# Token order of the activations, dropped meta columns, and the x rows at the start, in a one-layer hybrid mLSTM/HGRN2/RWKV-7 step

## The chip, the cores and the metric

The kernel runs on one core of one Trainium2 chip. The metric is the device time of one execution in microseconds (us). Engines are named as in the profile: PE is TensorE's matmuls, PEld its weight loads, DVE is VectorE, ACT ScalarE, POOL GpSimd, SP the queue from which all DMAs are issued.

## The reference

A layer is run over three streams of tokens: 64 sample tokens, 16 learned meta tokens that stand ahead of the prompt, and 512 prompt tokens. The width is 2048. Cut to what matters here:

```python
h = rmsnorm(x, p['norm_pre'])
proj = h @ p['w_in']                    # branches A (mLSTM), B (HGRN2), C (RWKV-7), and merge gates
ya, state = mlstm_branch(pa, ...)       # h * sigmoid(og) * silu(z), 8 heads
yb, state = hgrn_branch(pb, ...)        # 4 heads
yc, shift, state = rwkv_branch(pc, ...) # token shift, 8 heads of 64
ga, gb, gc = split_cols(jax.nn.sigmoid(f32(pg)), G_SIZES)
merged = ga * (ya @ w_proj_a) + gb * (yb @ w_proj_b) + gc * (yc @ w_proj_c)
y = merged @ p['w_out']
return x + rmsnorm(y, p['norm_post']), states
...
y_prompt = x_p[:, N_META:]              # the rows of the meta tokens are dropped
```

The meta tokens act on the recurrent states and on the shifted row of branch C. Their own gates, projections and output rows are computed by the reference and then dropped.

## The kernel before

The 592 tokens stand in the order sample (64), meta (16), prompt (512). **Activations** are kept transposed, `xh` and `xl`: 16 slices of 128 features by 592 tokens, split into a high part of type float32r and the rest. Each **tile** of weights is 128 output columns: `w_raw` (2 buffers) is loaded by SP, ACT makes `whi` (`split_hi`, L1130), DVE `wlo` (`split_lo`, L1445). `product(n)` (L641 to L658) multiplies a tile: for each of 16 slices k, three combinations (`whi`,`xh`), (`whi`,`xl`), (`wlo`,`xh`), and each in two halves of 296 tokens, which is 96 matmuls of 296 columns. The result lies in one of two accumulators of two banks (`acc`), columns 0 to 295 and 512 to 807; an ACT operation over both halves (`plain`, L1138) takes it out.

There are 154 tiles: 1 for the mLSTM gates, 1 for the RWKV ranks, then 8 for each of 8 mLSTM heads (key, value, query, output gate, z, three merge gate tiles), 8 for each of 4 pairs of RWKV heads (k, r, v, z, four gate tiles), 6 for each of 4 HGRN heads (forget, query, value, z, two gate tiles), 16 of the projections (L1093, three banks) and 16 of the output. Which small matmuls of the recurrences stand between or inside the products of a tile is written out by hand (`stages`, a plan of block numbers for RWKV and HGRN). Gate logits and branch rows are stored to DRAM and read again in the projection stage.

**Start.** SP issues the loads of 5 blocks of x rows, then two weight tiles. ACT squares and sums each block as it comes (L1149), then takes Ln (L1151) and Exp (L1153) for all five reciprocal roots; DVE makes five diagonal matrices of them (L1461, `unit`), and PE turns the rows by a float32 matmul with such a matrix (L679, 5 for each of 16 slices, in a ring of 4 PSUM buffers). ACT and DVE make `xh` (L1158) and `xl` (L1466) of each. ACT and DVE split weight tiles 0 and 1 ahead of that. The product of tile 0 starts when slice 12 of `xl` is there, and after all turning.

The names of the banks in the rows: `acc` are the accumulators, `branch` the two other PSUM tensors, `act_hi`/`act_lo` are `xh`/`xl`, `w_hi`/`w_lo` the split weights, `scratch` is everything carved out of one large tensor (the x rows and the recurrences' buffers).

## Time and profile before

| | |
|---|---|
| median of 3 runs (lowest, highest) | 2520.03 us (2518.99, 2521.3) |
| the profiled execution, its own time | 2519.03 us |
| its span | 2517.1 us |
| PE busy | 2417.9 us, 96% |
| PEld, DVE, ACT, POOL busy | 93%, 43%, 29%, 4% |
| DMA moved | 221 MB, 88 GB/s in the mean |

The page lists for each group of instructions the line, the engine, the operation, the tiles it writes and reads, the shapes, the count, and the busy time with the mean of one; the idle time behind it is what the engine waited just before. Spans of matmuls overlap, as they are pipelined, so the pace of a stream of matmuls is read from the starts in the timeline or from the chain, not from the length of one.

### The profile page before, as it was taken

Reading aid. Unit: us, or ns where it says so; the run is one execution under the profiler, and the core shown is the slowest. Engines: PE = TensorE matmul, PEld = TensorE weight load, DVE = VectorE, ACT = ScalarE, POOL = GpSimd, SP = SyncE. Lnnn points to the kernel's source line nnn. Section 1 sums busy time; section 2 is a strip of 40 time slices with the busy share of each in tenths; the row PEclk is TensorE's granted clock in tenths of the full one; section 3 lists DMA queues with packets and bytes.
Section 4 is the critical chain, followed back from the end, with each engine's and each line's share of the span. In section 5 each row is a group of like instructions: output and inputs, shape, how many; then the busy total and the mean of one; then the engine's idle time right before and its main releaser. Section 6 shows DMA issues by size and latency. Waiting matters only on the chain.

```text
span 2517.1 us, 46160 instructions
## 1 busy us (share of the span) xinstructions
PE 2417.9 (96%) x19469; PEld 2344.3 (93%) x19469; DVE 1081.0 (43%) x1616; ACT 726.1 (29%) x1019; POOL 103.2 (4%) x127
## 2 busy tenths in 40 slices
PE   6999999999999999999999999999999989999995
PEld 6999999999999999989989989898898989999995
DVE  3442324233242324735536445356656664444122
ACT  5222222122222212323233233232332343333231
POOL 0000000000000000000000000002202010000110
PEclk9999999999999999999999999999999989999998
DMA  4212222131322222112112121131121154433213
GB/s 160 86 60 102 84 82 106 50 115 62 104 74 96 84 89 90 51 45 99 42 55 86 45 85 56 45 135 68 71 96 68 50 176 138 148 109 135 82 67 119
DMA packets 50863, 221.18 MB, mean 88 GB/s; under 512 B 7363, under 2 KB 12661, under 8 KB 29173
## 3 DMA queue, kind: packets, MB, share of 16 engines
q1 hardware_dynamic: 50772, 219.80, 24.6%
q8 instruction: 78, 1.28, 0.2%
q14 instruction: 13, 0.10, 0.0%
HBM read 193.80 MB, written 25.98 MB: 87 GB/s over the span
## 4 chain that ended last, share of the span: by engine, by line
PE 82%; DVE 7%; issue 4%; ACT 3%; DMA 3%; SPq 1%; DVEq 0%; ACTq 0%
PE acc L656 61%; PE acc L1093 6%; PE branch L1093 2%; PE branch L832 2%; PE branch L870 2%; DMA w_raw<-in_w_stream 2%; DVE w_lo L1445 1%; ACT w_hi L1130 1%; DVE scratch L1927 1%; PE branch L825 1%; DMA scratch<-in_x_all 1%; DVE scratch L1926 1%; DVE scratch L1942 0%; PE branch L743 0%; DVE scratch L1663 0%
## 5 line engine op out<-in xcount | busy, mean ns | idle before, releaser
L656 PE MATMUL acc<-act_hi,w_hi 128*128 128x296 f32 x4416 | 992.5, 306 | 8.7 <-DVE act_lo L2017 3.5
L656 PE MATMUL acc<-act_hi,w_lo 128*128 128x296 f32 x4416 | 962.9, 299 | 0.0
L656 PE MATMUL acc<-act_lo,w_hi 128*128 128x296 f32 x4416 | 961.1, 299 | 0.0
L656 PEld LDWEIGHTS acc<-act_hi,w_hi 128*128 128x128 f32 x4416 | 712.4, 189 | 23.7 <-issue 10.9
L656 PEld LDWEIGHTS acc<-act_lo,w_hi 128*128 128x128 f32 x4416 | 719.0, 189 | 0.0
L656 PEld LDWEIGHTS acc<-act_hi,w_lo 128*128 128x128 f32 x4416 | 716.8, 188 | 0.0
L1445 DVE TENSOR_TENSOR w_lo<-w_raw,w_hi 128x2048 fp32r<-128x2048 f32 x154 | 354.0, 2299 | 836.5 <-ACT w_hi L1130 835.6
L1130 ACT ACTIVATE w_hi<-w_raw 128x2048 fp32r<-128x2048 f32 x154 | 294.3, 1912 | 219.3 <-PE branch L1093 142.1
L1138 ACT ACTIVATE gate_out<-acc 128x592 f32<-128x592 f32 x64 | 42.3, 662 | 314.5 <-PE acc L656 314.4
L1293 ACT ACTIVATE scratch<-branch 128x640 f32<-128x640 f32 x56 | 39.6, 707 | 217.5 <-PE branch L870 217.5
L1138 ACT ACTIVATE scratch<-acc 128x592 f32<-128x592 f32 x32 | 21.3, 665 | 261.7 <-PE acc L656 261.7
L1093 PE MATMUL acc<-act_hi,w_hi 128*128 128x296 f32 x384 | 85.1, 303 | 3.9 <-DVE act_lo L1989 3.9
L1093 PE MATMUL acc<-act_lo,w_hi 128*128 128x296 f32 x384 | 84.4, 301 | 0.0
L1093 PE MATMUL acc<-act_hi,w_lo 128*128 128x296 f32 x384 | 84.3, 301 | 0.0
L1643 DVE TENSOR_TENSOR scratch<-branch,masks 64x320 f32<-64x320 f32 (+1 forms) x72 | 44.5, 636 | 82.1 <-PE branch L832 44.2
L1093 PEld LDWEIGHTS acc<-act_hi,w_hi 128*128 128x128 f32 x384 | 63.4, 191 | 4.2 <-issue 4.2
L1093 PEld LDWEIGHTS acc<-act_lo,w_hi 128*128 128x128 f32 x384 | 63.6, 192 | 0.0
L1093 PEld LDWEIGHTS acc<-act_hi,w_lo 128*128 128x128 f32 x384 | 63.0, 191 | 0.0
L1022 PE MATMUL branch<-scratch 128*128 128x128 f32 (+1 forms) x312 | 40.0, 275 | 19.3 <-DVE scratch L1927 19.3
L832 PEld LDWEIGHTS branch<-scratch 64*64 64x64 f32 x1600 | 50.2, 134 | 8.7 <-issue 8.7
L1022 PEld LDWEIGHTS branch<-scratch 128*128 128x128 f32 (+1 forms) x312 | 36.1, 184 | 23.1 <-DVE scratch L1927 23.1
L832 PE MATMUL branch<-scratch 64*64 64x32 f32 x1600 | 54.2, 220 | 1.1
(396 smaller groups left out, 1940.3 us busy)
## 6 DMA issues: line engine op xcount, KB each, us to landing
w_raw<-in_w_stream SPq DMA_DIRECT2D x154, 1024.0 KB, 4.9
gate_logits<-gate_out SPq DMA_DIRECT2D x48, 296.0 KB, 2.2
scratch<-gate_logits SPq DMA_DIRECT2D x48, 296.0 KB, 3.3
scratch<-in_x_all SPq DMA_DIRECT2D x6, 1024.0 KB, 8.9
branch_rows<-branch_out SPq DMA_DIRECT2D x16, 296.0 KB, 2.1
scratch<-branch_rows SPq DMA_DIRECT2D x1, 2368.0 KB, 8.9
scratch<-branch_rows SPq DMA_DIRECT2D x2, 1184.0 KB, 6.5
w_raw<-in_x_all SPq DMA_DIRECT2D x2, 1024.0 KB, 5.7
```

What stands on the lines that cost most here:

```text
L656: last = mm(acc[s][:, 512 * h:512 * h + HALF], a[:, s, w], b[:, k, HALF * h:HALF * h + HALF], start=(k == 0 and a is whi and b is xh), sto ...
L825: last = mm(bank[:, P * c:P * c + P], lhs[r, span(c)], rhs[r, span(c)], start=True, stop=True)
L832: last = mm(bra[r, 512 * m + 32 * q:512 * m + 32 * q + 32], lhs[r, q, r], rhs(q, r), start=True, stop=True)
L870: last = turn(brb[:, P * c:P * c + P], src[:, 5 * h + c, :], ident)
L1022: last = mm(bank[0:LEN[c], P * c:P * c + LEN[c]], a[:, tok], b[:, tok], start=True, stop=True)
L1093: last = mm(banks3[b][:, 512 * h:512 * h + HALF], x[:, s, w], y[:, k, HALF * h:HALF * h + HALF], start=(k == ks[0] and x is whi and y is x ...
L1130: f(whi[:, s, :], wraw[:, s, :], ACT.Copy).then_inc(hi_done, 1)
L1138: f(split2(dst), source(n), ACT.Copy, scale=scale).then_inc(evac_done, 1)
L1293: S.done(f(dst[:, 5 * h:5 * h + 5, :].rearrange("p a b -> p (a b)"), brb[:, 0:5 * P], ACT.Copy), f"t{lv}_{h}")
L1445: v.tensor_tensor(wlo[:, s, :], wraw[:, s, :], whi[:, s, :].bitcast(F32), ALU.subtract).then_inc(lo_done, 1)
L1643: ins = v.tensor_tensor(out, a, b, op)
L1926: v.tensor_tensor(at(QK[lv % 2], 1), at(EE, 1), at(bq, 1), ALU.mult)
```

## The change

**Token order.** The order on the chip becomes sample (64), prompt (512), meta (16). A helper `given` cuts each block of x rows into the pieces that the inputs' order has. `product` takes a list of column ranges and works through the three combinations in one range and then in the other: `FULL_COLS` are all 592 tokens as 320 and 272, `QUERY_COLS` are 576 as 320 and 256, `EVEN_COLS` are 576 as 288 and 288. `FULL_COLS` stay for tiles 0 and 1, key and value of the mLSTM heads, the four first tiles of each RWKV pair, and forget and value of the HGRN heads: 2 + 16 + 16 + 8 = 42. `QUERY_COLS` are the 8 + 4 = 12 query tiles. `EVEN_COLS` are all the others: 5 x 8 + 4 x 4 + 3 x 4 + 16 + 16 = 100.

Where a branch needs its tokens in the old order, ACT takes them out of the accumulator in three operations (`placed`, 64, 16 and 512 columns; two for a query, whose meta columns are set to zero) in place of one. `shift_in` keeps its three, of other widths. Gates and branch rows are 576 wide, in the DRAM tensors too; the last block of x rows in the output stage has 64 rows and not 80.

**Start.** POOL computes the reciprocal root of each block as its sum comes, by an addition and a power. DVE scales the x rows of that block in place; the last block is scaled in two pieces, and `wlo` of the first 512 columns of weight tile 0 is made between them. PE turns rows by plain transposes: slices 0 to 2 ahead of tile 0, and slice k + 2 just ahead of the products of slice k. Tile 0 waits for `xl` of the slice at hand, and at slice 4 for the rest of its own `wlo`. The ring has 3 buffers. ACT and DVE split the rest of tile 0 after slices 2 and 3, and tile 1 after slices 8 and 9. The activation table for Exp is loaded at the beginning.

```diff
+FULL_COLS = ((0, 320, 0), (320, T, 576))
+QUERY_COLS = ((0, 320, 0), (320, KEPT, 576))
+EVEN_COLS = ((0, KEPT // 2, 0), (KEPT // 2, KEPT, 512))
...
-                        for h in range(2):
-                            last = mm(acc[s][:, 512 * h:512 * h + HALF], a[:, s, w], b[:, k, HALF * h:HALF * h + HALF],
+                    for lo, hi, at in cols:
+                        for a, b in ((whi, xh), (whi, xl), (wlo, xh)):
+                            last = mm(acc[s][:, at:at + hi - lo], a[:, s, w], b[:, k, lo:hi],
                                       start=(k == 0 and a is whi and b is xh), stop=(k == KT - 1 and a is wlo))
...
-                    product(n, at)
+                    product(n, at, cols=EVEN_COLS)
...
-            for k in range(KT):
-                if k >= 4:
-                    pe.wait_ge(x_lo, k - 3)
+            def turn_x(k):
+                if k >= 3:
+                    pe.wait_ge(x_lo, k - 2)
                 for t in range(5):
                     if k == 0:
-                        pe.wait_ge(x_unit, t + 1)
-                    last = mm(ring4[k % 4][:, P * t:P * t + ROWS[t]], xt[0:ROWS[t], t, P * k:P * k + P], unit[0:ROWS[t], t, 0:ROWS[t]], start=True, stop=True)
+                        pe.wait_ge(x_scaled, t + 1)
+                    elif k == 3 and t == 4:
+                        pe.wait_ge(x_scaled, 6)
+                    r = ROWS[t]
+                    last = turn(ring3[k % 3][:, P * t:P * t + r], xt[0:r, t, P * k:P * k + P], ident[0:r, 0:r])
                 last.then_inc(x_turned, 1)
-            product(0, {k: [lambda k=k: pe.wait_ge(x_lo, max(k, 12) + 1)] for k in range(0, KT)}, first=True)
+            pe.wait_ge(consts_here, 16)
+            for k in range(3):
+                turn_x(k)
+            first_stages = {}
+            for k in range(KT):
+                first_stages[k] = [lambda k=k: pe.wait_ge(x_lo, k + 1)]
+                if 1 <= k < KT - 2:
+                    first_stages[k].append(lambda k=k: turn_x(k + 2))
+            first_stages[4].append(lambda: pe.wait_ge(lo_done, 1))
+            pe.wait_ge(early_lo, 1)
+            product(0, first_stages, first=True, in_pieces=True)
             product(1, first=True)
...
-                product(N(2))
+                product(N(2), cols=QUERY_COLS)
                 turn_kv()
-                product(N(3))
+                product(N(3), cols=EVEN_COLS)
...
-            f(small[:, 8:13], small[:, 0:5], ACT.Ln, scale=1.0 / D, bias=eps[:, 0:1]).then_inc(x_sums, 1)
-            f(small[:, 16:21], small[:, 8:13], ACT.Exp, scale=-0.5).then_inc(x_sums, 1)
-            split_hi(0, first=True)
-            split_hi(1, first=True)
+            f(whi[:, 0, 0:EARLY_W], wraw[:, 0, 0:EARLY_W], ACT.Copy).then_inc(early_hi, 1)
             for k in range(KT):
                 act.wait_ge(x_turned, k + 1)
-                f(xh[:, k, :], ring4[k % 4][:, 0:T], ACT.Copy, scale=vec("norm_pre", k)).then_inc(x_hi, 1)
+                f(xh[:, k, :], ring3[k % 3][:, 0:T], ACT.Copy, scale=vec("norm_pre", k)).then_inc(x_hi, 1)
+                if k == 2:
+                    f(whi[:, 0, EARLY_W:D], wraw[:, 0, EARLY_W:D], ACT.Copy).then_inc(hi_done, 1)
+                elif k == 8:
+                    split_hi(1, first=True)
...
+                g.tensor_scalar(small[0:r, 8 + t:9 + t], small[0:r, t:t + 1], 1.0 / D, EPS, ALU.mult, ALU.add).then_inc(x_means, 1)
+                g.tensor_tensor(small[0:r, 16 + t:17 + t], small[0:r, 8 + t:9 + t], minus_half[0:r, :], ALU.pow).then_inc(x_rstd, 1)
```

PE's queue at the start of the program, before. L679 turns slices of x, L656 is the product:

```order
L679 MATMUL branch<-scratch 128x128 x4
L679 MATMUL branch<-scratch 128x80
L679 MATMUL branch<-scratch 128x128 x4
L679 MATMUL branch<-scratch 128x80
L656 MATMUL acc<-act_hi,w_hi 128x296 x2
L656 MATMUL acc<-act_lo,w_hi 128x296 x2
L656 MATMUL acc<-act_hi,w_lo 128x296 x2
```

The same place after it, where L710 turns a slice and L684 is the product:

```order
L710 MATMUL branch<-full,scratch 128x128 x4
L710 MATMUL branch<-full,scratch 128x80
L684 MATMUL acc<-act_hi,w_hi 128x320
L684 MATMUL acc<-act_lo,w_hi 128x320
L684 MATMUL acc<-act_hi,w_lo 128x320
L684 MATMUL acc<-act_hi,w_hi 128x272
L684 MATMUL acc<-act_lo,w_hi 128x272
L684 MATMUL acc<-act_hi,w_lo 128x272
L710 MATMUL acc<-full,scratch 128x128 x4
L710 MATMUL acc<-full,scratch 128x80
```

13 of the 16 turned slices have moved from ahead of tile 0 into it.

PE's queue in an mLSTM head, between the values inside a chunk (L736, L777) and tile 5 of the head, a merge gate; before:

```order
L736 MATMUL branch<-scratch 80x129
L736 MATMUL branch<-scratch 128x129 x4
L647 REGISTER_ALU
L656 MATMUL acc<-act_hi,w_hi 128x296 x2
```

After:

```order
L777 MATMUL branch<-scratch 80x129
L777 MATMUL branch<-scratch 128x129 x4
L675 REGISTER_ALU
L684 MATMUL acc<-act_hi,w_hi 128x288
L684 MATMUL acc<-act_lo,w_hi 128x288
L684 MATMUL acc<-act_hi,w_lo 128x288
```

The small matmuls and the count of the product's matmuls stay; the columns of each go from 296 to 288.

ACT's queue in the first tiles of an mLSTM head, before, where L1130 splits weights and L1138 takes a tile out of its accumulator:

```order
L1130 ACTIVATE w_hi<-w_raw 128x2048
L1134 REGISTER_ALU
L1138 ACTIVATE scratch<-acc 128x592
L1127 REGISTER_ALU
L1130 ACTIVATE w_hi<-w_raw 128x2048
```

After:

```order
L1173 ACTIVATE w_hi<-w_raw 128x2048
L1192 REGISTER_ALU
L1185 ACTIVATE scratch<-acc 128x64
L1187 ACTIVATE scratch<-acc 128x16
L1188 ACTIVATE scratch<-acc 128x512
L1170 REGISTER_ALU
L1173 ACTIVATE w_hi<-w_raw 128x2048
```

One operation has become three; no other work has moved on ACT there.

## Rows read from the trace of the kernel before

**Rows 1.** The page: span, busy times, and the group of ACT's weight splits.

```profile
span 2517.1 us, 46160 instructions
PE 2417.9 (96%) x19469; PEld 2344.3 (93%) x19469; DVE 1081.0 (43%) x1616; ACT 726.1 (29%) x1019; POOL 103.2 (4%) x127
...
L1130 ACT ACTIVATE w_hi<-w_raw 128x2048 fp32r<-128x2048 f32 x154 | 294.3, 1912 | 219.3 <-PE branch L1093 142.1
```

**Rows 2.** Waits of PE: who, for whom, us in total, times, longest.

```profile
...
PE branch L1022 <- DVE scratch L1927: 19.3, 16, 1.7
PE branch L1093 <- DVE scratch L2006: 4.3, 1, 4.3
PE acc L1093 <- DVE act_lo L1989: 3.9, 1, 3.9
PE acc L656 <- DVE act_lo L2017: 3.5, 1, 3.5
...
PE branch L688 <- ACT scratch L1172: 3.2, 1, 3.2
```

**Rows 3.** Timeline of PE in a product, full clock: start, length, instructions.

```profile
1002.33 0.43 PE L656 MATMUL acc<-act_lo,w_hi 128*128 128x296 f32 x2
...
1002.87 0.44 PE L656 MATMUL acc<-act_hi,w_hi 128*128 128x296 f32 x2
1003.15 0.43 PE L656 MATMUL acc<-act_lo,w_hi 128*128 128x296 f32 x2
```

**Rows 4.** PE at the granted clock 0.50: timeline, and a window of it.

```profile
75.97 0.70 PE L656 MATMUL acc<-act_hi,w_hi 128*128 128x296 f32 x2
...
76.96 0.70 PE L656 MATMUL acc<-act_hi,w_lo 128*128 128x296 f32 x2
...
75.60:78.90 3.30, 3.30 (x15) 3.30 (x14) 0.50 0.02 2
```

**Rows 5.** Timeline of PE, transposes between products.

```profile
115.82 0.71 PE L703 MATMUL branch<-full,scratch 128*80 128x128 f32 x5
116.37 0.27 PE L705 MATMUL branch<-full,scratch 128*128 128x128 f32 x1
```

**Rows 6.** The chain that ended last, 0 to 60 us: start, us, what.

```profile
3.82 14.74 DMA scratch<-in_x_all
18.58 2.00 ACT scratch L1149 x2
...
25.55 4.49 DVE w_lo L1445 x2
...
35.53 2.23 PE acc L679 x20
...
44.47 13.17 PE acc L656 x96
```

**Rows 7.** Timeline of ACT and DVE at three places of the start.

```profile
36.69 0.75 ACT L1158 ACTIVATE act_hi<-acc,vecs 128x592 fp32r<-128x592 f32 x1 [0.36 <-PE acc L679]
37.48 0.83 DVE L1466 SCALAR_TENSOR_TENSOR act_lo<-acc,vecs,act_hi 128x592 fp32r<-128x592 f32 x1 [0.28 <-ACT act_hi L1158]
...
73.91 0.23 ACT L333 ACTIVATE scratch<-acc 128x64 f32<-128x64 f32 x1
74.03 0.36 ACT L334 ACTIVATE scratch<-acc 128x232 f32<-128x232 f32 x1
...
77.28 0.46 DVE L1503 TENSOR_SCALAR low_acts<-low_acts 64x592 f32<-64x592 f32 x1 [0.77 <-ACT low_acts L1175]
```

**Rows 8.** Timeline of the second HGRN head, ACT and PE.

```profile
1791.07 0.67 ACT L1363 ACTIVATE scratch<-acc 128x592 f32<-128x592 f32 x1
...
1816.09 1.15 PE L1022 MATMUL branch<-scratch 128*128 128x128 f32 x8 [0.78 <-DVE scratch L1927]
```

**Rows 9.** The chain that ended last, from 2480 us on.

```profile
2496.69 5.57 DMA out_y_prompt<-scratch
2502.28 5.37 DMA scratch<-in_x_all
```

More of the change, by code:

```diff
@@ L58, in psum_col @@
 def psum_col(c):
-    return START[c] if c < 3 else 512 + START[c] - SPLIT
+    return [0, 64, 192, 576, 704][c]
 def part_col(c):
@@ L351, in build, with given @@
         x_junk = cv(D)
-        unit = cv(5 * P, 5, P)
         ROWS = [P] * 4 + [T - 4 * P]
-        ring4 = [acc[0], acc[1], bra, brb]
+        def given(t, rows):
+            pieces = []
+            for a, b, at in ((0, NS, 0), (NS, KEPT, C0), (KEPT, T, NS)):
+                lo, hi = max(a, P * t), min(b, P * t + rows)
+                if lo < hi:
+                    pieces.append((lo - P * t, hi - P * t, x_all[at + lo - a:at + hi - a, :]))
+            return pieces
+        X_LOADS = [len(given(t, ROWS[t])) for t in range(5)]
+        ring3 = [acc[1], bra, brb]
+        EARLY_W = 4 * P
         cv = Carver()
@@ L639, in _, with product @@
             turn = nc.tensor.transpose
-            def product(n, stages=None, first=False, unevacuated=0):
+            def product(n, stages=None, first=False, unevacuated=0, cols=FULL_COLS, in_pieces=False):
                 s = SLOT_OF(n)
                 stages = stages or {}
-                pe.wait_ge(lo_done, n + 1)
+                if not in_pieces:
+                    pe.wait_ge(lo_done, n + 1)
                 if not first:
@@ L747, in turn_h @@
                     pe.wait_ge(*vt.after(i, "h_unit"))
-                    for c in range(NCH):
+                    for c in (1, 2, 3, 4, 0):
                         o = psum_col(c)
-                        last = turn(brb[:, o:o + LEN[c]], hn[0:LEN[c], c, :], ident[0:LEN[c], 0:LEN[c]])
+                        n = P if c else NS
+                        last = turn(brb[:, o:o + n], hn[0:n, c, :], ident[0:n, 0:n])
                     pt.done(last, "h_turned")
@@ L1047, in turn_o @@
                     pe.wait_ge(*vt.after(i, "o_unit"))
-                    for c in range(NCH):
+                    for c in (1, 2, 3, 4, 0):
                         o = psum_col(c)
-                        last = turn(bra[:, o:o + LEN[c]], on[0:LEN[c], c, :], ident[0:LEN[c], 0:LEN[c]])
+                        n = P if c else NS
+                        last = turn(bra[:, o:o + n], on[0:n, c, :], ident[0:n, 0:n])
                     pt.done(last, "o_turned")
@@ L1061, in _ @@
                 for j in range(3):
-                    product(N(j))
+                    product(N(j), cols=QUERY_COLS if j == 1 else FULL_COLS)
                 products([N(3), N(4), N(5)],
@@ L1090, in _ @@
                             w = slice(P * k, P * k + P)
-                            for x, y in ((whi, xh), (whi, xl), (wlo, xh)):
-                                for h in range(2):
-                                    last = mm(banks3[b][:, 512 * h:512 * h + HALF], x[:, s, w], y[:, k, HALF * h:HALF * h + HALF],
+                            for lo, hi, at in EVEN_COLS:
+                                for x, y in ((whi, xh), (whi, xl), (wlo, xh)):
+                                    last = mm(banks3[b][:, at:at + hi - lo], x[:, s, w], y[:, k, lo:hi],
                                               start=(k == ks[0] and x is whi and y is xh), stop=(k == ks[-1] and x is wlo))
@@ L1134, in source, with plain, placed, in_order @@
                 act.wait_ge(tile_done, n + 1)
-                return halves(acc[SLOT_OF(n)])
-            def plain(n, dst, scale=1.0):
-                f(split2(dst), source(n), ACT.Copy, scale=scale).then_inc(evac_done, 1)
+                return halves(acc[SLOT_OF(n)], KEPT // 2)
+            def plain(n, dst):
+                f(split2(dst[:, 0:KEPT]), source(n), ACT.Copy).then_inc(evac_done, 1)
+            def placed(dst, src, func, rows=slice(0, P), meta=True, scale=1.0):
+                f(dst[:, 0:NS], src[rows, 0:NS], func, scale=scale)
+                if meta:
+                    f(dst[:, NS:C0], src[rows, 832:848], func, scale=scale)
+                return f(split2(dst[:, C0:T]), prompt_part(src)[rows], func, scale=scale)
+            def in_order(n, dst, scale=1.0, meta=True):
+                act.wait_ge(tile_done, n + 1)
+                placed(dst, acc[SLOT_OF(n)], ACT.Copy, meta=meta, scale=scale).then_inc(evac_done, 1)
+            nc.scalar.preload_act_table_set("exp_and_others")
             S = S0["setup_scalar"]
@@ L1349, in _ @@
                 S.done(f(khat, khat, ACT.Exp), "end_exp")
-                plain(N(2), bv)
+                in_order(N(2), bv)
                 split_hi(N(4))
@@ L1386, in _ @@
                 act.wait_ge(y_here[0 if k < EARLY else 1 if k < NH_A + NP_C else 2], 16)
-                f(xh[:, k, :], YIN[:, place[k], :], ACT.Copy).then_inc(y_hi, 1)
+                f(xh[:, k, 0:KEPT], YIN[:, place[k], :], ACT.Copy).then_inc(y_hi, 1)
             act.wait_ge(*E_["shift_tensor"].after(0, "shift_turned"))
@@ L1868, in _ @@
                 split_lo(N(1))
+                v.memset(bq[:, NS:C0], 0.0)
                 col = dve.snap(i + VEC["lb"])
```

199 lines of the change are left out of this document (112 added, 87 removed).

## The prediction

> **What bounds the kernel now.** I read the page's busy times first, then the waits of PE, then the timeline inside a product, then the chain at both ends. PE is busy 96% of the span, and its weight loads 93% [rows 1]; DVE and ACT have more than half of theirs free. The waits of PE behind its first instruction are few: 19.3 us in the HGRN heads on DVE, 4.3 + 3.9 + 3.5 us where the projection and output stages begin, 3.2 us on ACT in the set-up [rows 2]. So from tile 0 to the last tile a microsecond taken out of PE's work is a microsecond of the kernel, save where one of those waits takes it back. The product makes up most of that work: tile 0 takes 13.17 us for 96 matmuls, 137 ns each [rows 6], and a tile in the middle shows the same: six matmuls pass between 1002.33 and 1003.15 us [rows 3]. 154 tiles make 14784 such matmuls, 2028 us of 2517. The rest is small matmuls, which keep their shapes but for a few columns, and the two ends: 44.47 us before tile 0 starts [rows 6], and what follows the last tile, where output and x rows pass in turn [rows 9].
>
> **Narrower tiles.** 112 of the 154 tiles (100 even, 12 query) lose 16 of their 592 columns, in 48 pairs of matmuls each: 112 x 48 x 16 = 86016 columns fewer. The 42 others keep 592 columns, as 320 + 272. What is a column worth? The trace has one width for this kind of matmul, so I bound it. At the half clock two matmuls follow two others after 0.495 us, 247 ns each [rows 4], which is 296 columns at 1.2 GHz to the nanosecond: there a column costs one cycle and nothing else is seen. At the full clock of 2.4 GHz, one cycle per column is 0.417 ns and 123 ns for 296; the measured 137 has 14 ns on top. If those are fixed, a column is worth 0.417 ns: 35.8 us. If they grow with the width, it is worth 137 / 296 = 0.463 ns: 39.8 us. No row is nearer to one than to the other, so I take 0.44: **37.8 us**. Can a weight load hold the pace instead? Five float32 transposes with 128-column loads start within 0.55 us, 110 ns each [rows 5]; a load of that size and type of operand fits into 110 ns, less than the 119 to 134 ns that the narrower matmuls need. So mostly no; what is left of it is in the rivals.
>
> The order inside a slice also changes: three matmuls on one range, then three on the other. Each had its own load before too (19469 of both [rows 1]), and the rows of a product step on evenly whether the next pair has a new weight or the old one [rows 3]. I cost it at nothing; the cover is that loads run beside the matmul before, and without it each pair would pay tens of ns.
>
> **What takes some of it back.** In an HGRN head ACT takes the z tile out at 1791.07, and from there a chain on DVE with ACT decides until the last wait of L1022 at 1816.09 [rows 8]. PE's products in that stretch (18 slices of 6 matmuls, 8 columns less, 0.38 us) end earlier for nothing; with the shorter wait behind it about 0.45 us a head, 1.8 us in four. The three waits at the stage starts end by data or by DMA; the tile ahead of the 4.3 us wait gives its 0.3 us back. In all **-2.1 us** (0 to -4). Elsewhere the trace of PE shows no wait, and the plan by block numbers leaves DVE and ACT a step that shrinks by 8 x 6 x 0.44 = 21 ns a slice. ACT's three operations for one: the 64-column piece starts the next one 0.12 us later [rows 7], so a tile is out some 0.2 us later. The accumulator is needed one whole tile (13 us) later and split weights likewise; on the path this is nothing. Where it does stand on the path, in the set-up chain from tile 0 to the wait on L1172 (3.2 us [rows 2]), six small operations for two cost **-0.2 us** (0 to -1). PE waits there in any case, and that chain starts with tile 0's end, so what the start gains is kept.
>
> **The start.** Before: the last x rows land at 18.56 us, ACT's sum ends at 20.6, tables, roots, two split tiles and 16 slices of turning follow, and tile 0 runs from 44.47 to 57.6 us [rows 6]. After, I lay the steps out again. 20.6: last sum. Two small POOL operations and the first piece of scaling on DVE: no row has a power on POOL; DVE takes 592 columns in 0.46 us [rows 7], so 1.0 us in all (0.6 to 3). DVE then makes 512 columns of `wlo` (a quarter of 4.49 / 2, 0.6 us [rows 6]) and scales the other 1664 columns (2.8 x 0.46, 1.3 us at most), and makes slice 0 of `xl` (0.83 us [rows 7]): 24.4 us with the hand-overs. ACT's share runs beside it. From there PE has 13.17 us of products and 13 turned slices. A slice was 2.23 / 20 x 10 = 1.12 us of ten float32 matmuls [rows 6]; a plain transpose is one matmul of 110 ns, five are 0.55 us: 7.1 us. PE has been idle, so it begins at the half clock, where a slice's six products take 1.48 us in place of 0.82: 2.0 us (0 to 3). ACT needs 0.75 us and DVE 0.83 for a slice of which PE makes one in 1.37, so they follow, but not while they split weight tile 1 (1.9 us [rows 1] and 2.2 us [rows 6]) with only three buffers in the ring: 2.5 us (0 to 4). Tile 0 ends at 24.4 + 13.2 + 7.1 + 2.0 + 2.5 = 49.2 us, **8.4 us** earlier (5 to 12). Tile 1 follows at once in both. SP has two more DMAs for x rows to issue ahead of the weights; the bytes are the same, and tile 0's weights are first needed behind the last x rows, so I cost that at nothing (0 to 1 us late).
>
> **The end.** The last x rows are loaded only when the first output has left: 5.57 us, then 5.37 us of load [rows 9]. That load falls from 80 rows to 64 and the last store likewise, while the first store grows from 48 prompt rows to 64: **0.5 us** (0 to 1.5).
>
> **Sum.** 37.8 - 2.1 - 0.2 + 8.4 + 0.5 = 44.4 us from the profiled execution's 2519.0 us, 2474.6; the median of the runs is 1.0 us above that execution: **2475.6 us**. The half clock is granted for a few microseconds behind each long wait of PE [rows 4]; where such a stretch falls is not settled by the code, so 3.4 us either way. Low end: 39.8, nothing taken back, 12 at the start: some 2467. High end of this case: 35.8 - 4 - 1 + 5: 2484.
>
> **Rivals.**
> *The start runs slow.* PE stays at the half clock through tile 0, or ring and splits hold it: 96 x 110 ns and 13 x 0.55 us are 17.7 us at most, so the start gives nothing or takes 9 us: 2484 to 2494. For it: in tile 0 transposes and waits stand between every slice's products. Against it: transposes between products run at 110 ns [rows 5], the full pace. The Trainium skill (TensorE: Matmul & The Clock Gate, PE-mode transpose) says that transposes do not count as activity for the clock; by that rule this is the case that comes, if it holds for a third of transposes among two thirds of matmuls. Chance 0.11.
> *The loads set the pace.* The load stays 128 columns wide. If 137 ns is the pace of load and hand-over, the width between 256 and 320 is free, and only start and end are left: 2511. For it: PEld is busy 93% [rows 1], and 137 is more than the columns need. Against: 110 ns with the same load [rows 5]. The Trainium skill (same page, Back-to-back issue gap) has both instructions of a pair set the spacing, 81 ns at 128 columns and 131 at 512; its slope would make 86016 columns worth 11 us, but this trace has 137 ns at 296 already, so I do not take its figures. Chance 0.05.
> *A floor, and wide halves that pay: slower.* If 137 ns is a floor for this kind of matmul below 296 columns, while above it each column costs 0.44 ns, the narrow tiles give nothing and each 320-column matmul costs 10.6 ns more: 54 tiles x 48 x 10.6 ns = 27.5 us against 8.9 - 0.2 from the ends: 2539. With a lower floor the narrow ones begin to gain; the two sides cancel at 135.4 ns. For it: the unexplained 14 ns. Against: [rows 5] and, at the half clock, a pace that is the columns alone [rows 4]. Chance 0.03.
>
> **How the numbers follow.** The forecast's case has 0.81. The range is 2467 to 2490: it holds that case and about half of the slow start. 0.2%, 5 us, is what a measurement of this kernel can tell from no change. Faster by more: the first two cases and nearly all of the third, 0.95; within it 0.02; slower 0.03.
>
> **What would show it.** The trace of after should have product matmuls of 288 columns at 133 to 134 ns, 320 at 147 to 148, 272 at 126 to 127, so 12.8 us for an even tile; tile 0 ending near 49 us; HGRN waits some 2 us longer in sum; PE's small matmuls unchanged. Wrong would be 288-column matmuls at 137 ns, a granted clock of 0.50 through tile 0, or new waits of PE on ACT's take-out.

## The result, and the profile after

The changed kernel takes 2493.47 us (median of 4 runs, 2491.66 to 2494.59) where the kernel before took 2519.51 in the same session: ratio 0.9895, 95% interval 0.9878 to 0.9912, some 26 us faster. 2475.6 was forecast, with 2467 to 2490 as range. The direction was right and the size was not: 18 us are missing, and the time lies outside the range.

The page of after, to be held against [rows 1]: span, busy times, the queue of the code's own transfers, and the product's first group.

```profile
span 2490.6 us, 46093 instructions
PE 2377.3 (95%) x19389; PEld 2298.0 (92%) x19389; DVE 1083.4 (43%) x1626; ACT 724.4 (29%) x1088; POOL 106.8 (4%) x139
...
q8 instruction: 140, 2.29, 0.4%
...
L684 PE MATMUL acc<-act_hi,w_hi 128*128 128x288 f32 (+1 forms) x4416 | 1341.2, 304 | 23.6 <-issue 8.2
```

PE is busy 40.6 us less than before, more than was gained: its busy share fell, so it waits more. The waits of PE say with whom (engine, line, for whom: us in total, times, longest), to be held against [rows 2]:

```profile
PE branch L1064 <- DVE scratch L1993: 18.0, 14, 1.9
PE acc L684 <- issue: 8.2, 6, 1.9
PE acc L684 <- DVE w_lo L1501: 6.4, 7, 1.3
PE acc L684 <- ACT gate_out L1181: 5.4, 4, 1.4
PE branch L1136 <- DVE scratch L2073: 4.7, 1, 4.7
```

The list of before has these three further down, which the prediction did not count:

```profile
PE branch L1050 <- DVE scratch L1978: 3.4, 4, 0.9
...
PE acc L656 <- DVE w_lo L1445: 2.8, 7, 0.6
PE acc L656 <- issue: 2.4, 3, 0.9
```

So the wait for `issue` has grown from 2.4 to 8.2 us, and that of a product for `gate_out` is new. All seven new waits of these two kinds, 10.9 us, lie at one kind of place: between the last product of one mLSTM head and the first of the next. PE's timeline there, second head (start us, length, instruction, in brackets the idle time and what the profile puts it down to):

```profile
182.40 0.29 PE L684 MATMUL acc<-act_lo,w_hi 128*128 128x288 f32 x1
182.53 0.29 PE L684 MATMUL acc<-act_hi,w_lo 128*128 128x288 f32 x1
184.17 0.41 PE L684 MATMUL acc<-act_hi,w_hi 128*128 128x320 f32 x1 [1.35 <-ACT gate_out L1181]
184.42 0.31 PE L684 MATMUL acc<-act_lo,w_hi 128*128 128x320 f32 x1
184.57 0.31 PE L684 MATMUL acc<-act_hi,w_lo 128*128 128x320 f32 x1
```

1.64 us from start to start where 0.13 is the pace. It comes seven times, at every step from one head to the next (184.17, 297.77, 412.49, 525.67, 638.82, 752.51, 867.71 us; 1.62 to 2.15 us each); in the mLSTM heads of the kernel before there is none of it. Behind three of them PE is granted half its clock for 3.4 us (columns: stretch, its length, PE busy with count, granted clock, DMA share, GB/s):

```profile
299.20:302.60 3.40, 3.40 (x16) 0.50 0.63 169
753.20:756.60 3.40, 3.40 (x17) 0.50 0.56 166
869.20:872.60 3.40, 3.40 (x17) 0.50 0.67 176
```

From the first tile of the first mLSTM head to the end of the last the kernel before takes 912.6 us and this one 911.5: where the narrower tiles should have brought 16 us, it gained one. The queue named "instruction" in the page is the other new thing: 140 packets in place of 78, 2.29 MB in 140, so 16 KB each. Asked for the stretch of the heads alone (176 us to the end of that loop), its row is, first of before and then of after:

```profile
q8 instruction: 1, 0.02, 0.0%
```

```profile
q8 instruction: 64, 1.05, 0.6%
```

So before, the code of the loop was loaded once; after, it is loaded again in every head, nine pieces a head. PE's gap begins where it comes round to the loop's first instruction.

The kernel before had the same sign in another place. Its three waits for `issue` stand where one RWKV pair ends and the next begins, and in its last three pairs (1149 us to 1635 us) the queue's row is

```profile
q8 instruction: 44, 0.72, 0.6%
```

That loop has some 3360 instructions and is loaded again in every turn, before and after.

The other steps of the forecast can be read off. A column costs what the forecast had as its upper bound: products start 0.13 us apart at 288 columns, 0.15 at 320, and 0.115 at 256:

```profile
1749.44 0.28 PE L684 MATMUL acc<-act_lo,w_hi 128*128 128x256 f32 x1
1749.55 0.28 PE L684 MATMUL acc<-act_hi,w_lo 128*128 128x256 f32 x1
1750.94 0.42 PE L684 MATMUL acc<-act_hi,w_hi 128*128 128x320 f32 x1 [1.11 <-DVE w_lo L1501]
1751.19 0.31 PE L684 MATMUL acc<-act_lo,w_hi 128*128 128x320 f32 x1
1751.34 0.31 PE L684 MATMUL acc<-act_hi,w_lo 128*128 128x320 f32 x1
...
2067.26 0.29 PE L1136 MATMUL acc<-act_hi,w_lo 128*128 128x288 f32 x1
2067.39 0.29 PE L1136 MATMUL acc<-act_hi,w_hi 128*128 128x288 f32 x1
```

Over whole stages the medians are 118, 125, 132, 136 and 147 ns for 256, 272, 288, 296 and 320 columns: 0.46 ns a column and nothing beside it. The third row is also the HGRN head's wait between its second and third tile, 1.39 us from start to start, 0.73 before.

The start, against [rows 6] (the chain that ended last: start, us, what):

```profile
5.03 14.63 DMA scratch<-in_x_all
19.68 2.01 ACT scratch L1205 x2
...
21.77 0.20 POOL small L2129
...
22.04 0.55 POOL small L2131
...
25.52 1.82 PE acc L684 x6
```

The last x rows are summed from 19.68 us on and not from 18.58; tile 0 begins at 25.52 (24.4 forecast) and ends at 52.07 (49.2 forecast, 57.5 before). That start gained 5.4 us, not 8.4.

### The profile page after: what moved, and what is told of

It reads as the page before. It is cut to its first block, busy times and chain, and to the rows that moved or that the text cites. A ratio compares the mean times of both kernels' runs of the same rounds, so it can differ in the third digit from the quotient of the medians.

```text
span 2490.6 us, 46093 instructions
## 1 busy us (share of the span) xinstructions
PE 2377.3 (95%) x19389; PEld 2298.0 (92%) x19389; DVE 1083.4 (43%) x1626; ACT 724.4 (29%) x1088; POOL 106.8 (4%) x139
## 3 DMA queue, kind: packets, MB, share of 16 engines
q8 instruction: 140, 2.29, 0.4%
## 4 chain that ended last, share of the span: by engine, by line
PE 83%; DVE 7%; issue 4%; ACT 3%; DMA 2%; SPq 1%; DVEq 0%; ACTq 0%; POOL 0%
PE acc L684 62%; PE acc L1136 6%; PE branch L1136 2%; PE branch L874 2%; PE branch L912 2%; DVE w_lo L1501 1%; DVE scratch L1993 1%; DMA w_raw<-in_w_stream 1%; PE branch L867 1%; ACT w_hi L1173 1%; DMA scratch<-in_x_all 1%; DVE scratch L1992 1%; DVE scratch L1955 1%; PE branch L784 0%; DVE scratch L2008 0%
## 5 line engine op out<-in xcount | busy, mean ns | idle before, releaser
L684 PE MATMUL acc<-act_hi,w_hi 128*128 128x288 f32 (+1 forms) x4416 | 1341.2, 304 | 23.6 <-issue 8.2
L684 PE MATMUL acc<-act_lo,w_hi 128*128 128x288 f32 (+1 forms) x4416 | 1312.0, 297 | 0.0
L684 PE MATMUL acc<-act_hi,w_lo 128*128 128x288 f32 (+1 forms) x4416 | 1310.7, 297 | 0.0
L684 PEld LDWEIGHTS acc<-act_hi,w_hi 128*128 128x128 f32 x4416 | 836.4, 189 | 40.4 <-issue 17.7
L684 PEld LDWEIGHTS acc<-act_lo,w_hi 128*128 128x128 f32 x4416 | 835.9, 189 | 0.5
L684 PEld LDWEIGHTS acc<-act_hi,w_lo 128*128 128x128 f32 x4416 | 836.1, 189 | 0.0
L1181 ACT ACTIVATE gate_out<-acc 128x576 f32<-128x576 f32 x64 | 41.5, 649 | 300.0 <-PE acc L684 299.9
L1136 PE MATMUL acc<-act_hi,w_hi 128*128 128x288 f32 x384 | 113.8, 296 | 4.4 <-DVE act_lo L2056 4.4
L1136 PE MATMUL acc<-act_lo,w_hi 128*128 128x288 f32 x384 | 114.0, 297 | 0.0
L1136 PE MATMUL acc<-act_hi,w_lo 128*128 128x288 f32 x384 | 113.7, 296 | 0.0
L1349 ACT ACTIVATE scratch<-branch 128x640 f32<-128x640 f32 x56 | 39.6, 707 | 214.6 <-PE branch L912 214.6
L1136 PEld LDWEIGHTS acc<-act_hi,w_hi 128*128 128x128 f32 x384 | 72.8, 190 | 4.9 <-issue 4.1
L1136 PEld LDWEIGHTS acc<-act_hi,w_lo 128*128 128x128 f32 x384 | 73.0, 190 | 0.0
L1136 PEld LDWEIGHTS acc<-act_lo,w_hi 128*128 128x128 f32 x384 | 72.7, 189 | 0.0
```

The costliest lines, as they stand in the source:

```text
L684: last = mm(acc[s][:, at:at + hi - lo], a[:, s, w], b[:, k, lo:hi], start=(k == 0 and a is whi and b is xh), stop=(k == KT - 1 and a is wlo))
L1136: last = mm(banks3[b][:, at:at + hi - lo], x[:, s, w], y[:, k, lo:hi], start=(k == ks[0] and x is whi and y is xh), stop=(k == ks[-1] and ...
L1181: f(split2(dst[:, 0:KEPT]), source(n), ACT.Copy).then_inc(evac_done, 1)
L1349: S.done(f(dst[:, 5 * h:5 * h + 5, :].rearrange("p a b -> p (a b)"), brb[:, 0:5 * P], ACT.Copy), f"t{lv}_{h}")
```

## The experiments

Each kernel below was timed against the kernel before on the same chip; differences are taken from the time of before in that session (2517.63 for e1 to e4, 2518.44 for e5 to e8, 2519.20 for e9 to e11 and 2519.11 us for e12 to e14; 2519.51 for the changed kernel). Where two changed kernels of different sessions are compared, the gap between their times can be off by the 2 us that these differ. Where more than time is said, it is from the run's trace.

**Is it the supply of code?** The new start turns x by 80 transposes where there were 80 float32 products. The page counts them: 19469 matmuls and as many weight loads before [rows 1], 19389 of each now, since such a product is two pairs and a transpose one. So PE's stream ahead of the mLSTM loop is 160 instructions shorter, and 14 waits longer; the loop itself has the same number as before. One experiment puts the 146 back by waits for a count that was reached long before, of which two make one instruction; the other shifts the kernel before by the amount that leads to the same place in a piece of 16 KB, with 220 such waits ahead of its turning loop. Of e1:

```diff
+            for _ in range(292):
+                pe.wait_ge(vecs_here, 16)
             pe.wait_ge(consts_here, 16)
```

> The changed kernel with 146 more instructions at the head of TensorE's stream (waits for a count that was reached long before, run while TensorE is idle at the start). They put back the shift of the code: 80 float32 products of four instructions each became 80 turnings of two each, 160 fewer, and 14 waits came in. Nothing else differs, also not in what is computed. Theory 1, instruction supply (the mLSTM loop's code lies across one more piece of what is fetched at a time, and no longer stays in place from one head to the next): no gap of 1.6 to 2.1 us at the start of a new head, the half-clock stretches behind three of them gone, instruction packets down from 140 to about 80, and 2493.5 less 14 to 18 us: 2476 (2472 to 2481). Theory 2, the gap comes from the work at the loop's end (ScalarE's placed take-out, the last waits of the head): all of it stays, 2493 (2491 to 2496).

Measured: 2478.26 us (2476.69 to 2479.16), ratio 0.9845 (0.9828 to 0.9861). That is 15.2 us below the changed kernel, or 13.3 if each is taken against the before of its own session, by nothing but idle waits. In the traces the mLSTM heads take 894.7 us in place of 911.5.

> The kernel before with 110 more such instructions at the head of TensorE's stream, which is 146 less than 256 and so puts its mLSTM loop at the same place in a piece of 16 KB as the changed kernel's, with none of the change in it. Theory 1, instruction supply: a gap of about 1.6 us at seven head starts and some half-clock stretches behind them, about 140 instruction packets in place of 78, and 2519.5 plus 13 to 18 us: 2535 (2530 to 2539). Theory 2, the gap belongs to what the change does at the loop's end: no effect, 2519.5 (2518 to 2522).

Measured: 2532.22 us (2530.28 to 2534.2), ratio 1.0055 (1.0039 to 1.0072): 14.6 us slower than the kernel before, with none of the change in it. The instruction queue in the page of e1 and in that of e2:

```profile
q8 instruction: 78, 1.28, 0.2%
```

```profile
q8 instruction: 141, 2.31, 0.4%
```

PE's timeline in e2 at the second head:

```profile
191.65 0.43 PE L656 MATMUL acc<-act_hi,w_lo 128*128 128x296 f32 x2
193.40 0.54 PE L656 MATMUL acc<-act_hi,w_hi 128*128 128x296 f32 x2 [1.32 <-ACT gate_out L1140]
```

And a whole head, the third, of after and of e1 (stretch, its length, then busy time and count of PE, PEld, DVE, ACT, POOL, granted clock, DMA share, GB/s):

```profile
297.70:412.40 114.70, 113.37 (x832) 111.36 (x832) 36.75 (x67) 25.65 (x32) 1.36 (x2) 0.99 0.24 86
```

```profile
294.30:405.80 111.50, 111.50 (x833) 109.71 (x833) 36.77 (x67) 25.65 (x32) 1.37 (x2) 1.00 0.25 88
```

The head of e1 has no idle time of PE at all, 3.2 us less than after's with the same instructions. In e1 all seven gaps are gone and no half clock is granted between 74 and 1674 us. In e2 all seven are there, 1.56 to 2.06 us, and one stretch of half clock. The profile puts e2's gap down to `gate_out`, too, though ScalarE's take-out is what it always was in that kernel: the name is that of the last wait that PE passed, and not the cause. Theory 1 holds in both directions, and theory 2 falls in both.

**Which places are good?** Two runs without repetition, 98 and 194 instructions instead of 146.

> The changed kernel with 98 more instructions at TensorE's head, not 146: the mLSTM loop begins 48 instructions earlier than in the kernel before. Working estimate: the loop is about 1,700 instructions of 64 bytes, 6.6 pieces of 16 KB; it lies across seven pieces for some 97 of the 256 starting places and across eight for the others, and stays in place only at seven. A span of 97 places around the kernel before's, wherever it lies in it, holds the place 48 earlier or the place 48 later, one and not both. So this run or its partner shows 78 instruction packets and 2478, and the other 140 and 2493. Rival: what counts is another measure (the length of the head alone, or all pieces up to the loop's end), and both or neither are slow.

Measured: 2502.16 us and 141 packets.

> Partner of the run with 98: 194 more instructions at TensorE's head, so the mLSTM loop begins 48 later than in the kernel before. One of the two shows about 78 instruction packets and 2478 us, the other about 140 and 2493 us; by the rival both or neither are slow.

Measured: 2478.49 us and 78 packets. One and not both, as expected of a loop of 6.6 pieces that stays in place across seven and not across eight. The 6.6 is an estimate: 832 matmuls and 832 loads a head in the rows above and some 30 others, at 256 instructions a piece. The slow one is slower than the changed kernel (2502, not 2493): after six of its seven steps from head to head a second gap of 0.9 to 1.7 us follows some 3 us behind the first, in the first tile. So the code's place decides whether it is fetched again, and also how many of the fetches come late.

The Trainium skill (Runtime: NRT & Kernel Launch, Instruction fetch mechanics) gives TensorE's store as 128 KiB, refilled in blocks of 16 KiB or 256 instructions. The runs agree with the blocks: 16 KB a packet, and 110 instructions forward doing what 146 back do. Of the size they show less: by the estimate above the loop was kept over seven blocks and lost over eight, although eight of 16 KB make 128. The same section says that the prefetch is purely sequential, so that a branch out of a window of two pages has to fetch its target. Here the runs differ: at seven blocks e1 fetches no piece from 176 to 960 us, which holds the seven returns to the loop's start.

**The parts alone.** e3 is the token order with the start of the kernel before, e4 the new start in the old token order; their streams ahead of the loop are as long as before's and as after's. The core of e3's edit, TensorE's side (`unit` is made from `ident` and the roots as in the kernel before):

```diff
-                    last = turn(ring3[k % 3][:, P * t:P * t + r], xt[0:r, t, P * k:P * k + P], ident[0:r, 0:r])
+                    last = mm(ring4[k % 4][:, P * t:P * t + ROWS[t]], xt[0:ROWS[t], t, P * k:P * k + P], unit[0:ROWS[t], t, 0:ROWS[t]], start=True, stop=True)
```

> The changed kernel with the start of the kernel before: x rows not scaled as they arrive, turned by products with scaled diagonals ahead of tile 0, both first weight tiles split whole. The token order and the narrower tiles stay. TensorE's stream ahead of the mLSTM loop is then as long as in the kernel before. Theory 1, instruction supply: the head-start gaps are gone although the token order is in: 2519.5 less 26.5 (saved in all) less 17 (the gaps) plus 5.4 (what the new start had won) is 2481 (2477 to 2486), faster than the changed kernel. Theory 2, the gaps belong to the token order's take-outs: they stay, and the kernel loses the start's 5.4 us: 2499 (2497 to 2502).

Measured: 2486.48 us (2483.61 to 2486.89), ratio 0.9873 (0.9857 to 0.989); 78 packets, no gaps. The token order and narrower tiles alone beat the whole change by 7 us (5 against each session's before), because they leave the head of the stream alone. It is 5.5 us behind the expectation, though. Tile 0 begins at 46.80 us where it began at 44.27: the token order itself costs at the start.

> The kernel before with the new start alone (x rows scaled as they arrive, plain turnings between the products of tile 0, first weight tile in two pieces); tokens in the old order, all tiles 592 columns wide. Theory 1, instruction supply: the start gains about 5 us and the shorter head of TensorE's stream costs 13 to 18 us in the mLSTM loop: 2519.5 - 5 + 16 = 2530 (2526 to 2534), slower than the kernel before, with about 140 instruction packets. Theory 2: only the start's gain, 2514 (2512 to 2516).

Measured: 2521.63 us (2519.66 to 2524.68), ratio 1.0017 (1.0007 to 1.0026); 140 packets, and seven gaps of 1.5 to 2.0 us. The new start, made to save time, gives 9.1 us by the end of tile 0 and loses 13.2 us in the eight heads of its trace. It is slower than nothing, by less than expected, since no half clock followed its gaps and its start gained 9 us and not 5.

> The kernel before with the new start alone (old token order, all tiles 592 wide, x rows in five whole blocks), and the 146 instructions at TensorE's head that put the mLSTM loop back. It is what the start is worth with neither the loop's loss nor the token order's loads. Theory: the unpadded one began its second tile 9.1 us earlier than the kernel before and lost the gain at the heads' starts; now the gain stays, and 2518.5 - 9 = 2509.5 (2508 to 2511), with about 78 instruction packets. Rival: the start's gain is taken back in the set-up behind tile 1: 2514 to 2518.

Measured: 2510.93 us (2509.05 to 2511.27), ratio 0.9968 (0.9954 to 0.9981), 78 packets: the start alone is worth 8.2 us, the forecast's 8.4.

**What the token order costs at the start.** A block of x rows in the new order comes from two places, so blocks 0 and 4 are loaded in two pieces each. Same kernel as e12, with the pieces and without the order:

```diff
-                sp.dma_start(xt[0:ROWS[t], t, :], x_all[P * t:P * t + ROWS[t], :]).then_inc(x_here[t], 16)
+                for a, b in X_PIECES[t]:
+                    sp.dma_start(xt[a:b, t, :], x_all[P * t + a:P * t + b, :]).then_inc(x_here[t], 16)
```

> The same kernel, still in the old token order, with x's first row block loaded as two transfers of 64 rows and the last as 64 and 16 rows: the pieces of the token order, without the order. Theory: a packet of 8 KB takes 309 ns in a block of 128 rows and 520 to 640 ns in the token order's pieces, so the last x rows land 2 to 3 us later and all moves by it: the run above plus 2.5 us (1.5 to 3.5). Rival: the pieces cost nothing by themselves, and the late rows come from the order (source rows 80 and up, the changed tiles): the same time as the run above.

Measured: 2512.65 us (2511.38 to 2513.86), ratio 0.9974 (0.9963 to 0.9984): 1.7 us more by the medians, and tile 0 ends 2.3 us later in the trace. The bytes moved in 0.4 us steps from 2 to 18 us say why, first of e12, then of e13:

```profile
GB/s 191 41 123 451 389 348 451 451 269 451 428 430 348 430 451 410 430 471 410 410 430 471 369 410 492 389 430 451 410 328 287 225 205 266 205 164 246 205 328 430
```

```profile
GB/s 97 287 41 0 205 328 246 164 246 225 266 184 246 169 110 241 300 410 471 410 410 451 369 492 410 410 451 430 430 410 410 492 389 430 430 389 246 246 164 225
```

Whole blocks of 128 rows run at some 430 GB/s; the two pieces of 64 rows at some 210, for the first 5 us; the last block of 80 rows, which was one transfer before, runs at that rate in both. All the engines are busy all the while: a packet of 8 KB takes 309 ns in a whole block and 440 to 640 ns in the pieces. Three cures were tried on it.

> The changed kernel with the 146 instructions ahead and x's first row block loaded by one transfer of 128 rows (rows 0 to 63 and 80 to 143, as two groups a fixed distance apart) in place of two of 64 rows; the same rows in the same partitions. With the two pieces the first slices of the load ran at about 200 to 240 GB/s for some 5 us, where the kernel before and the new start alone show 414 and more from the third slice on. Theory: a transfer that fills 64 partitions goes at about half the rate, and tile 0 starts later by the whole of it (the old start in token order began its tile 0 at 46.80 and not at 44.27 us): now tile 0 begins about 2.3 us earlier and the time is 2478.3 - 2.3 = 2476 (2475 to 2477). Rival: the rows are late because of ScalarE's squares and GpSimd's powers, not the transfer: 2478 unchanged.

Measured: 2503.65 us (2502.65 to 2504.68). The one transfer, `x_all` seen as two groups of rows, was moved by a tenth of the engines, at 55 GB/s in the end, and tile 0 ended 26 us later than in e1. The test failed, and tells another thing. The Trainium skill (DMA: Bandwidth & Descriptors, Why a DMA increments its semaphore by 16 and not by 1) has a transfer from this queue use no more engines than its outermost dimension divides by, here two of 16; the busy share of a tenth agrees.

> The changed kernel with the 146 instructions ahead; of the first x row block the second piece of 64 rows, and both pieces of the last block, are issued by ScalarE's queue at its start, while SyncE's queue issues the rest in the old order. (The one transfer in two groups moved its block at some 55 GB/s, a tenth of the engines busy, and so tested another thing than meant.) Theory: in the changed kernel all 16 engines were busy at 200 to 240 GB/s while only 64 partitions were being filled; with the other 64 filled at the same time the load runs at 400 or more from the start, the x rows are all there 2 to 3 us earlier, and tile 0 begins that much earlier: 2478.3 - 2.5 = 2475.8 (2474.5 to 2477). Rival: a transfer of 64 rows is slow in itself, whatever runs beside it, or the rows are not what tile 0 waits for: 2478 (2477 to 2480).

Measured: 2477.48 us (2475.97 to 2479.27), the same time as e1's within what can be told between sessions, with tile 0 beginning 1.3 us later in the trace and ending 2.9 us later. The load of the x rows ran at 115 to 307 GB/s for nearly 10 us during which ScalarE's queue had a piece under way, whole blocks beside it included. The theory fell in this form: two halves at a time are no faster than one after the other.

> The changed kernel with the 146 instructions and the HGRN split behind the reciprocals (2471.7), and each transfer of the first and the last x block cut in two by columns, so in packets of 4 KB. Theory 1, the 64 partitions being filled are the limit: a packet of half the size takes half of the long time, and the load and the kernel stay as they are, 2472 (2470 to 2474). Theory 2, the number or the size of a transfer's packets is the limit: the early slices of the load change, to above 300 GB/s if short packets help (2469 to 2470) or below 200 if they hurt (2474 to 2477).

Measured: 2471.92 us (2470.4 to 2472.29) against 2471.66 of the same kernel without the cut (e10, below). Packets of 4 KB took 256 to 320 ns, half of the long time of 8 KB, and the rate stayed at 170 to 244 GB/s: it hangs on the bytes to these partitions and not on the packets. The Trainium skill (SBUF — State Buffer, Door 1: The DMA port swizzle) says just that: partitions 0 to 63 reach one half of the 16 ports and 64 to 127 the other. For one piece at a time the traces agree, 210 for 430. The further transfers that SP has to issue are not the cost: four more of them here moved tile 0's begin by 0.7 us and its end by 0.1. Why two at once on both halves stayed slow (e9) is not shown by any run.

**The HGRN heads.** VectorE's order in front of the third tile, in after (start, us, instruction):

```profile
1739.56 3.85 DVE L1954 RECIPROCAL scratch<-scratch 128x592 f32<-128x592 f32 x1
1743.33 3.79 DVE L1955 RECIPROCAL scratch<-scratch 128x592 f32<-128x592 f32 x1
1747.15 0.53 DVE L1957 TENSOR_SCALAR scratch<-scratch 128x592 f32<-128x592 f32 x1
1747.60 0.58 DVE L1958 TENSOR_SCALAR scratch<-scratch 128x592 f32<-128x592 f32 x1
1748.22 0.47 DVE L1960 TENSOR_SCALAR scratch<-scratch 128x592 f32<-128x592 f32 x1
1748.60 2.28 DVE L1501 TENSOR_TENSOR w_lo<-w_raw,w_hi 128x2048 fp32r<-128x2048 f32 x1
```

`w_lo`, for which PE waits from 1749.7 us on, stands last behind the gate's chain, and the chain starts with ScalarE's take-out, now six operations for two. First (e6) the split was put ahead of everything, and on ScalarE `split_hi(N(2))` ahead of the take-out. On VectorE:

```diff
+                split_lo(N(2))
                 dve.wait_ge(evac_done, N(0) + 1)
...
                 V.done(v.tensor_scalar(bef, bef, 1e-19, None, ALU.max), "f")
-                split_lo(N(2))
```

> The changed kernel with the 146 instructions ahead, and in the HGRN loop the split of the third tile's weights ahead of the first tile's take-out on ScalarE and ahead of the gate's two reciprocals (3.85 us each) on VectorE. In the changed kernel TensorE waits 1.38 us between the second and third tile of each head (0.73 before). Theory, the lower half of the weights is late because the six placed take-outs delay the gate's chain that stands ahead of it on VectorE: the wait goes, 4 x 1.2 = 4.8 us less, unless the gate's chain, now some 2.3 us later, is waited for further on: 2473.5 (2472 to 2476). Rival, the gate's chain is what later work of the head hangs on: the wait moves to the turning of the keys, and the time is 2478 to 2482.

Measured: 2475.9 us (2475.12 to 2476.05), ratio 0.9831 (0.9815 to 0.9848). Against e1, heads 1 to 3 gain 1.4 us each, but head 0 loses 4.8, so by the traces the four together lose 0.6 and the lower time is not theirs (between tile 1 and the second mLSTM head e6 is 1.2 us shorter, see below). In head 0 the third tile's weights have only just landed, the gate's chain now stands behind them on VectorE, and the split of the fourth tile behind the chain. The third tile's split on VectorE in head 0, with its own wait, and PE's waits from 1628 to 1666 us:

```profile
1629.73 2.29 DVE L1503 TENSOR_TENSOR w_lo<-w_raw,w_hi 128x2048 fp32r<-128x2048 f32 x1 [14.41 <-ACT w_hi L1175]
```

```profile
PE acc L684 <- DVE w_lo L1503: 4.1, 2, 3.2
```

Next (e10) ScalarE was left as in after, and the split put behind the reciprocals:

```diff
                 V.done(v.reciprocal(bep, bep), "f2")
+                split_lo(N(2))
...
                 V.done(v.tensor_scalar(bef, bef, 1e-19, None, ALU.max), "f")
-                split_lo(N(2))
```

> The changed kernel with the 146 instructions ahead; in the HGRN loop VectorE's split of the third tile's weights is moved ahead of the three operations behind the two reciprocals, and ScalarE's order is as in the changed kernel. With the split ahead of all of the gate's chain the wait fell from 1.38 to 0.13 us in heads 1 to 3, but in head 0, where the third tile's weights landed 9.5 us after the first tile's end, the chain stood behind that load and TensorE lost 4.3 us. Theory: behind the reciprocals the split finds its weights there in every head; 1.0 to 1.2 us less in each of four heads: 2478.3 - 4.4 = 2474 (2473 to 2475.5). Rival: the three operations and the logarithm behind them, 2.3 us later, are waited for by the turning of the keys: 2477 to 2480.

Measured: 2471.66 us (2471.1 to 2472.43), ratio 0.9811 (0.9796 to 0.9826). The wait is gone in every head but the first, where 1 us of it stays, and PE steps from the second tile into the third without a break:

```profile
1731.21 0.28 PE L684 MATMUL acc<-act_hi,w_lo 128*128 128x256 f32 x1
1731.33 0.31 PE L684 MATMUL acc<-act_hi,w_hi 128*128 128x320 f32 x1
1731.48 0.31 PE L684 MATMUL acc<-act_lo,w_hi 128*128 128x320 f32 x1
```

**Together.**

> The changed kernel with the three edits together: 146 instructions ahead of TensorE's stream, x's pieces on two queues, the HGRN split behind the reciprocals. If each theory holds they add, since they lie in different stages: 2478.3 - 2.5 - 4.4 = 2471.4 (2469.5 to 2473.5). If the pieces gain nothing: 2474; if the HGRN order gains nothing: 2476.

Measured: 2474.48 us (2473.68 to 2475.38), the number forecast for pieces that gain nothing. Against e10, timed in the same session, they cost 2.8 us; the trace has tile 0 end at 53.84 us, 3.2 us later than e10's. The best version is e10: the changed kernel, 146 idle instructions at the head of TensorE's stream, and one split moved. It is 47.5 us (1.9%) faster than the kernel before and 22 us faster than the changed one.

## Why the prediction was wrong, point by point

**"From tile 0 to the last tile a microsecond taken out of PE's work is a microsecond of the kernel, save where one of those waits takes it back."** This is the step that failed. It counts waits that the trace of before shows, and the loss was one that it doesn't show: the mLSTM loop's code stayed in place only because of where it began. The one hint, 2.4 us of `issue` at the turns of the RWKV loop, was on the list and was passed over. The change took 146 instructions out ahead of it. I costed the change's instructions by their time and not by their number. Price: 15.2 us of time (2493.5 to 2478.3 in e1; 13.3 against each session's before), 14.6 with the sign turned (e2), and 16.8 in the mLSTM heads of the traces. This is most of the 18 us. With it set right, e1 lies inside the range, 2.7 us above the forecast; its gain over before, 39.4 us, is 5.0 short of the forecast's 44.4.

**Narrower tiles, 37.8 us.** Right in kind, and its upper bound was the truth: 0.46 ns a column, 86016 columns, 39.6 us of PE's work. An even tile takes 12.69 us (12.8 forecast). The rivals of a pace set by loads and of a floor are out: 256 columns take 118 ns.

**Take-back, 2.1 us, and "a tile is out some 0.2 us later ... on the path this is nothing".** Too small, and "Elsewhere the trace of PE shows no wait" was a misreading: 2.8 us for `w_lo` and 3.4 us at L1050 were on the list. From the first HGRN head to the first projection tile before takes 407.2 us and e1 406.4. The 16 narrower tiles there are worth 5.7 us (12288 columns at 0.46 ns), so 4.9 were taken back where 1.8 was forecast. In an HGRN head the fifth and the sixth tile keep nothing of their 0.4 us each (0.01 gained and 0.17 lost), where half of that was forecast, and the wait ahead of the third tile grew from 0.73 to 1.39 us; the four waits in the sixth tiles (L1050, now L1093) grew from 3.4 to 4.2 us in all. The take-out is on the path ahead of the third tile, because the gate's chain and then `w_lo` follow it; for the fifth and sixth tile that is argued and no run shows it. e10 gives 6.6 us by the medians of two sessions and 4.3 by the traces, more than the wait had grown, as the 0.73 us of before go with it.

**The start, 8.4 us.** As a term of the new start it was right: 8.2 us in e12, 8.4 in its trace at tile 0's end. The two stalls for tile 1's splits are 0.8 and 1.6 us in after from start to start, 2.5 forecast. The mis-sized term is "SP has two more DMAs for x rows ... 0 to 1 us late": the pieces cost 2.3 us in e13's trace, 2.5 in e3's. The bytes were the same, the rate was not. The rival of a slow start did not come: the granted clock was 0.50 to 29.5 us and for one more stretch of 3.4 us from 43.2, and 1.00 between, where transposes stand among products. That second stretch makes up most of the rest of what after's start lacks: its tile 0 takes 26.5 us, and e1's, without the stretch, 25.0 (24.8 forecast).

**The set-up chain, 0.2 us.** From tile 1's start to the second head e1 takes 131.8 us, 1.2 us more than e6 and e9: there a half-clock stretch of 3.4 us falls into PE's wait, and in e1 one of 6.8 reaches beyond it. That is the 3.4 us either way of the forecast.

**The end, 0.5 us.** What follows the last product takes 30.83 us before and 30.27 after, 0.6 less where 0.5 was forecast.

## What to carry to other kernels

Look at the page's instruction queue, and at waits for `issue` where a loop turns, before an edit to a loop that just fits or ahead of it, and count instructions ahead of the loop as well as in it: a float32 product is twice a transpose here. If an edit that removes work makes a far loop slower, or a gap stands at the step from one turn to the next with an engine named that had long been done, shift the code by idle instructions in both directions before you look for another cause. And a split of a transfer by partitions is not free when the bytes stay the same.

## What was not expected of the hardware

A loop of some 6.6 pieces of 16 KB on TensorE runs with no fetch at all at some places (78 packets in the whole program) and with nine a turn at others (140), and pays 1.8 to 3.0 us a turn for it (e4, e7). Nothing lies between these two in any run here. The RWKV loop, some 13 pieces by the same estimate, is fetched again in before, after and e1 alike, 43 or 44 packets in its last three turns, and PE takes 1.1 to 1.5 us from start to start at each turn; the HGRN loop, 5.6 pieces, is not fetched again in before or e1.

The half clock follows gaps of this size only at times (3 of 7 in after, 1 of 7 in e2, 0 of 7 in e4 and in e7), in stretches of 3.4 us, and makes a product of 320 columns take 267 ns.

A transfer that fills 64 of 128 partitions runs at 210 GB/s and not 430, and slows those that run beside it (e9); one whose outermost dimension is two runs at a tenth of the engines.
